# The first modulation of a two-block transformer kernel: shift half as direct products on TensorE, scale half on VectorE, and the first scaling ahead of the shift coefficient

## The reference, cut to what matters

```python
c_act = jax.nn.silu(c)                                          # (1, 1024)
mod = jnp.split(c_act @ w_ada[0] + b_ada[0], 9, axis=-1)        # mod[0] is the shift, mod[1] the scale, 1024 each
h = rms_norm(x, ffn1_norm[0]) * (1 + mod[1][:, None, :]) + mod[0][:, None, :]
x = x + 0.5 * (1 + mod[2])[:, None, :] * swiglu(h, ffn1_w_gu[0], ffn1_w_down[0])
```

## Time and profile before

| | us |
|---|---|
| median of 3 runs | 3137.26 (3135.42 to 3139.18) |
| profiled execution | 3139.89 |
| its span | 3138.1 |
| PE busy | 3095.8 |
| DVE busy | 1816.2 |
| ACT busy | 1201.4 |
| POOL busy | 1017.5 |

### The profile page before, as it was taken

One profiled execution on the slowest core, in us unless ns is written; L12 is line 12 of the kernel. 1 busy time (PEld: TensorE's weight loads), 2 busy tenths in 40 slices (PEclk: granted clock), 3 DMA queues, 4 the chain that ended last, 5 costly groups with the idle time before them and its releaser, 6 DMA issues.

```text
span 3138.1 us, 39389 instructions
## 1 busy us (share of the span) xinstructions
PE 3095.8 (99%) x14397; PEld 2511.1 (80%) x14397; DVE 1816.2 (58%) x2456; ACT 1201.4 (38%) x1818; POOL 1017.5 (32%) x722
## 2 busy tenths in 40 slices
PE   6999999999999999999999999999999999999999
PEld 5888877788888888877788888777888788888887
DVE  6555476665546443376665556446777868575443
ACT  4333246432223222246432234455433342443332
POOL 4995000069911830000079810000799101040000
PEclk8999999999999999999999999999999999999999
DMA  6665334267633643332266634212666345343332
GB/s 242 206 204 156 92 89 125 74 195 207 203 100 120 204 123 97 93 89 74 74 195 207 204 96 135 68 54 68 201 207 199 102 127 110 94 142 97 97 94 94
DMA packets 581129, 420.43 MB, mean 134 GB/s; under 512 B 41717, under 2 KB 541252, under 8 KB 579864
## 3 DMA queue, kind: packets, MB, share of 16 engines
q1 hardware_dynamic: 542116, 287.93, 31.4%
q0 software_dynamic: 35456, 124.01, 13.5%
q10 hardware_dynamic: 3444, 7.02, 0.8%
HBM read 413.10 MB, written 8.68 MB: 134 GB/s over the span
## 4 chain that ended last, share of the span: by engine, by line
PE 93%; DVE 4%; ACT 1%; issue 1%; DMA 1%; SPq 0%; DVEq 0%; ACTq 0%
PE bank L327 28%; PE bank L329 28%; PE bank L328 28%; PE bank L1574 2%; PE bank L1588 1%; PE bank L1615 1%; DVE w_lo L308 1%; PE bank L363 1%; PE bank L365 1%; PE bank L364 1%; DMA mod_w<-in_w_ada 1%; DVE tmp L457 1%; DVE h_lo L467 0%; PE bank L3136 0%; PE bank L417 0%
## 5 line engine op out<-in xcount | busy, mean ns | idle before, releaser
L327 PE MATMUL bank<-h_hi,w_hi 128*128 128x512 f32 x2624 | 1035.8, 395 | 4.9 <-DVE h_lo L467 3.1
L329 PE MATMUL bank<-h_hi,w_lo 128*128 128x512 f32 x2624 | 1023.8, 390 | 0.0
L328 PE MATMUL bank<-h_lo,w_hi 128*128 128x512 f32 x2624 | 1023.2, 390 | 0.0
L308 DVE TENSOR_TENSOR w_lo<-raw,w_hi 128x1024 fp32r<-128x1024 f32 x414 | 609.4, 1472 | 567.3 <-ACT w_hi L291 564.9
L291 ACT ACTIVATE w_hi<-raw 128x1024 fp32r<-128x1024 f32 x414 | 437.7, 1057 | 788.4 <-PE bank L329 788.3
L327 PEld LDWEIGHTS bank<-h_hi,w_hi 128*128 128x128 f32 x2624 | 492.1, 188 | 122.4 <-issue 10.9
L329 PEld LDWEIGHTS bank<-h_hi,w_lo 128*128 128x128 f32 x2624 | 492.0, 187 | 105.8
L328 PEld LDWEIGHTS bank<-h_lo,w_hi 128*128 128x128 f32 x2624 | 492.6, 188 | 100.4 <-issue 0.5
L760 POOL TENSOR_TENSOR mod_acc<-mod_acc,mod_w 128x1024 f32<-128x1024 f32 x168 | 446.8, 2659 | 14.7
L327 PE MATMUL bank<-hid_hi,w_hi 128*128 128x512 f32 (+1 forms) x1068 | 415.6, 389 | 3.9 <-DVE w_lo L308 3.3
L329 PE MATMUL bank<-hid_hi,w_lo 128*128 128x512 f32 (+1 forms) x1068 | 413.3, 387 | 0.0
(11 more groups left out here) (433 smaller groups left out, 3279.6 us busy)
## 6 DMA issues: line engine op xcount, KB each, us to landing
raw<-in_ffn_w_gu SPq DMA_DIRECT2D x176, 512.0 KB, 4.4
mod_w<-in_w_ada POOLq DMA_DIRECT2D x128, 512.0 KB, 3.9
mod_w<-in_mod_w POOLq DMA_DIRECT2D x96, 512.0 KB, 4.2
raw<-in_ffn_w_in SPq DMA_DIRECT2D x88, 512.0 KB, 3.8
raw<-in_ffn_w_down SPq DMA_DIRECT2D x64, 512.0 KB, 3.5
raw<-in_w_in SPq DMA_DIRECT2D x34, 512.0 KB, 3.7
raw<-in_ffn_w_out SPq DMA_DIRECT2D x32, 512.0 KB, 3.5
raw<-in_ffn_w_down SPq DMA_DIRECT2D x32, 384.0 KB, 3.1
```

Of the source, the lines that this page charges most:

```text
L308: loop(nc.vector.tensor_tensor(w_lo[:, u % 2, :], raw[:, u % 2, :], w_hi[:, u % 2, :].bitcast(F32), ALU.subtract), "split_lo", times)
L327: nc.tensor.matmul(dst, a_hi, b_hi, start=start, stop=False)
L328: nc.tensor.matmul(dst, a_hi, b_lo, start=False, stop=False)
L329: return nc.tensor.matmul(dst, a_lo, b_hi, start=False, stop=stop)
```

## The change

It does five things. (1) DVE accumulates only columns 1024 to 2047 of each chunk, the scale half. (2) The shift half of each chunk is multiplied on PE as it is: mod_direct makes 8 products of one column, with mod0_w as weights and cact[t] as the column, and adds them up over the chunks in bank 6. PE does chunks 0 to 4, norm_spread, chunks 5 and 6, the scale sums (mod_total), chunk 7, and then pe_later. (3) SP loads the last chunk in two halves, the scale half first; the shift half waits for chunk 0 to have landed, since it uses that chunk's semaphore. (4) DVE scales tile 0 between the scale coefficient and the shift coefficient; one of the two first split_lo stands between them, the other behind the first h_lo; DVE is one scaling ahead of its h_lo instead of two. ACT waits for the shift coefficient before its first rounding. (5) FIRST_PAIR has (1, 0) second instead of third.

```diff
--- before.py
+++ after.py
@@ -581,7 +581,7 @@
                     done(ins, "unit_used")
             turn.pe += 2
 
-        FIRST_PAIR = [(0, 0), (0, 1), (1, 0), (0, 2), (1, 1), (0, 3), (1, 2), (0, 4), (1, 3), (0, 5), (1, 4), (0, 6), (0, 7),
+        FIRST_PAIR = [(0, 0), (1, 0), (0, 1), (0, 2), (1, 1), (0, 3), (1, 2), (0, 4), (1, 3), (0, 5), (1, 4), (0, 6), (0, 7),
                       (1, 5), (1, 6), (1, 7)]
 
         def first_pair_pe(pe, key):
@@ -601,6 +601,8 @@
 
             for m in range(n):
                 wait(act, "norm_scaled", (key, m))
+                if key == PHASES[0] and m == 0:
+                    act.wait_ge(sg.sem("coef_ready"), at("coef_ready", "shift"))
                 done(nc.scalar.activation(dst_hi(m), tmp[:, m % 3, :], ACT.Identity,
                                           bias=0.0 if shift is None else shift(m)), "norm_hi", (key, m))
 
@@ -642,13 +644,20 @@
         def set_parts(key, s):
             return [j for t, j in mod_jobs(key) if t == s]
 
-        def mod_total(pe, s, j, bank):
+        def mod_direct(pe, t, j, bank, first):
+
+            for b in range(KT):
+                ins = nc.tensor.matmul(psum[bank][:, 8 * j + b:8 * j + b + 1], mod0_w[:, t, j * D + b * P:j * D + (b + 1) * P],
+                                       cact[:, t:t + 1], start=first and b == 0, stop=False, skip_group_check=True)
+            return ins
+
+        def mod_total(pe, s, j, bank, alone=True):
 
             wait(pe, "mod0_summed", (s, j))
             for b in range(KT):
                 ins = nc.tensor.matmul(psum[bank][:, 8 * j + b:8 * j + b + 1],
                                        mod_acc[:, j * D + b * P:j * D + (b + 1) * P], ones[:, 0:1],
-                                       start=True, stop=True, skip_group_check=True)
+                                       start=alone, stop=True, skip_group_check=True)
             done(ins, "mod_total", (s, j))
 
         def folds(n):
@@ -782,9 +791,13 @@
                 sp.dma_start(x_tok[:, t, :], d["x"][0, t * P:(t + 1) * P, :]).then_inc(sg.sem("x_loaded"), 16)
             wait(sp, "rows_cleared", "all")
             load_rows(sp, True)
-            for t in range(KT):
+            for t in range(KT - 1):
                 sp.dma_start(mod0_w[:, t, :], d["w_ada"][0, t * P:(t + 1) * P, 0:2 * D])\
                     .then_inc(sg.sem(f"mod0_loaded{t}"), 16)
+            last = d["w_ada"][0, (KT - 1) * P:KT * P, 0:2 * D]
+            sp.dma_start(mod0_w[:, KT - 1, D:2 * D], last[:, D:2 * D]).then_inc(sg.sem(f"mod0_loaded{KT - 1}"), 16)
+            sp.wait_ge(sg.sem("mod0_loaded0"), 16)
+            sp.dma_start(mod0_w[:, KT - 1, 0:D], last[:, 0:D]).then_inc(sg.sem("mod0_loaded0"), 16)
 
         def load_rows(sp, first):
             name = "rows_first" if first else "rows_loaded"
@@ -853,10 +866,16 @@
                     ins = nc.tensor.transpose(psum[m % 2][:, t * P:(t + 1) * P], x_tok[:, t, m * P:(m + 1) * P],
                                               ident[:, :])
                 done(ins, "x_turned", m)
-            norm_spread(pe, PHASES[0], 4)
+            wait(pe, "act_c", "c")
+            for t in range(KT - 1):
+                pe.wait_ge(sg.sem(f"mod0_loaded{t}"), 16)
+                mod_direct(pe, t, 0, 6, t == 0)
+                if t == 4:
+                    norm_spread(pe, PHASES[0], 4)
+            mod_total(pe, 0, 1, 3)
+            pe.wait_ge(sg.sem("mod0_loaded0"), 32)
+            done(mod_direct(pe, KT - 1, 0, 6, False), "mod_total", (0, 0))
             pe_later(pe)
-            mod_total(pe, 0, 1, 3)
-            mod_total(pe, 0, 0, 6)
 
         def pe_later(pe):
 
@@ -894,26 +913,24 @@
             take_rows(0)
             wait(dve, "shape_loaded", "all")
             wait(dve, "act_c", "c")
-            acc = mod_acc[:, 0:2 * D]
-            for t in range(KT - 1):
+            acc = mod_acc[:, D:2 * D]
+            for t in range(KT):
                 dve.wait_ge(sg.sem(f"mod0_loaded{t}"), 16)
                 if t == 0:
-                    ins = nc.vector.tensor_scalar(acc, mod0_w[:, t, :], cact[:, t:t + 1], None, ALU.mult)
+                    ins = nc.vector.tensor_scalar(acc, mod0_w[:, t, D:2 * D], cact[:, t:t + 1], None, ALU.mult)
                 else:
-                    ins = nc.vector.scalar_tensor_tensor(acc, mod0_w[:, t, :], cact[:, t:t + 1], acc, ALU.mult, ALU.add)
-                vstep(ins)
-                if t == 5:
+                    ins = nc.vector.scalar_tensor_tensor(acc, mod0_w[:, t, D:2 * D], cact[:, t:t + 1], acc, ALU.mult, ALU.add)
+                if t < KT - 1:
+                    vstep(ins)
+                else:
+                    done(ins, "mod0_summed", (0, 1))
+                if t == 3:
                     norm_invert(dve, PHASES[0])
-            t = KT - 1
-            dve.wait_ge(sg.sem(f"mod0_loaded{t}"), 16)
-            for j in (1, 0):
-                half = acc[:, j * D:(j + 1) * D]
-                done(nc.vector.scalar_tensor_tensor(half, mod0_w[:, t, j * D:(j + 1) * D], cact[:, t:t + 1], half, ALU.mult,
-                                                    ALU.add), "mod0_summed", (0, j))
-            for _ in range(LOOK):
-                split_lo(dve)
             mod_coef(dve, 0, [1], 3)
+            norm_scale(dve, PHASES[0], psum[4][:, :], 0, lambda m: x[:, m, :], gain_of(0))
+            split_lo(dve)
             mod_coef(dve, 0, [0], 6)
+            mark("coef_ready", "shift")
 
         def take_rows(t):
             n = 1 if t == 0 else ROW_TILES - 1
@@ -1350,8 +1367,13 @@
             kind, l = FFN[key]
             s = key[1]
             if key not in LAZY:
-                norm_scale_split(dve, key, 4, KT, lambda m: x[:, m, :], gain_of(s), shift_of(s),
-                                 lambda m: h_lo[:, m, :], lambda m: h_hi[:, m, :])
+                dst_lo, dst_hi = lambda m: h_lo[:, m, :], lambda m: h_hi[:, m, :]
+                for m in range(1, KT):
+                    norm_scale(dve, key, psum[4][:, :], m, lambda m: x[:, m, :], gain_of(s))
+                    norm_low(dve, key, m - 1, shift_of(s), dst_lo, dst_hi)
+                    if m == 1:
+                        split_lo(dve)
+                norm_low(dve, key, KT - 1, shift_of(s), dst_lo, dst_hi)
                 after_norm(dve)
             u0 = turn.dve - LOOK
             mark("pair_evac", (key, "base"))
```

## The result

| | before | after |
|---|---|---|
| median | 3137.57 us (11 runs) | 3146.0 us (11 runs) |
| ratio, 95% interval | | 1.0022 (1.0014 to 1.003) |
| profiled execution, its span | 3139.89, 3138.1 | 3143.53, 3141.7 |
| DVE busy | 1816.2 | 1794.3 |
| matrix instructions of PE | 14397 | 14509 |

The change makes the kernel slower by 8.4 us by the medians (9.1 in the second series; the ratios say 7 and 9); 10 was forecast. Ten of the eleven runs after lie between 3142.5 and 3149.4; one execution of 13919 us at a granted clock of 0.21 is a disturbance that the ratio leaves out.

A forecast was written before the change was run, and what follows sets the result against it. PE, busy for 99% of the span, was taken to bound the kernel. First dense product at 54.3 instead of 43.75 (+10.5), clock -0.5, all else 0: +10.0 on the median, 3147.3 us, range 3142 to 3151.5.

The forecast's parts named there:

- The step that was taken as deciding: PE's direct products: half clock from 21.9, 0.218 us per instruction, 3.5 us per chunk against loads every 2.5 us.
- (1): DVE's accumulation of w_ada chunks: half as wide, some 1.2 us saved per chunk, counted 0 because PE is not ready.
- (2): PE's 64 direct products replacing 8 sums: last direct product ends at 51.1, where the last sum ended at 40.8.
- (3): pe_later on PE: no longer hidden, its 3.2 us stand behind the last direct product and end at 54.3.
- (4): Tile 0 scaled before the shift coefficient: first h_lo 1.6 us after it instead of 2.3; gain 0.7 covered, counted 0.
- (5): New waits and queues on ACT and SP: cost 0; next raw loads land 4.4 us later, hidden.
- (6): Clock of the first dense products: half-clock stretch may shorten or lengthen, taken as -0.5 us, bounds -2.7 and +2.7.
- Rival A: PE keeps full clock through the direct products, last one at 37.4: result -5, 3132 us; chance 0.06.
- Rival B: Full clock lasts three to seven us longer on PE's direct products: +4 to +7, 3141 to 3144 us; chance 0.08.
- C: Direct products dearer beside DMA traffic, or half clock after 54.3 twice as long: +12 to +14, 3150 to 3152; chance 0.06.

The follow-up runs named there:

- direct3: The changed kernel with direct products for the first 3 chunks only, DVE summing the other shift chunks, norm_spread and pe_later ahead of the sums: 3136.97 us, ratio 0.9995 to before.
- direct5: The changed kernel with direct products for the first 5 chunks only, DVE summing the other shift chunks, norm_spread and pe_later ahead of the sums: 3142.13 us, ratio 1.0012 to before.
- direct_dense2: The changed kernel with two float32 products of 512 columns among each chunk's 8 direct products, 16 in all: 3147.35 us, ratio 1.0033 to before.
- after_again: The changed kernel itself, run once more in the second series: 3146.01 us, ratio 1.0028 to before.
- later_first: The changed kernel with pe_later moved from behind the last direct product to ahead of the scale sums: 3148.91 us, ratio 1.0037 to before.
- scale_first: The kernel before with only parts 4 and 5 of the change (DVE and ACT order, FIRST_PAIR): 3137.39 us, ratio 0.9997 to before.
- direct_filled: The changed kernel with 7 transposes of the identity into an unused bank among each chunk's 8 direct products: 3148.9 us, ratio 1.0035 to before.
- direct_dense: The changed kernel with one float32 product of 384 columns into an unused bank among each chunk's 8 direct products: 3156.36 us, ratio 1.0056 to before.
- dense_scale_first: The kernel before with scale_first's edit and PE's idle time filled with 10, 2 and 2 float32 products of 512 columns: 3133.53 us, ratio 0.9989 to before.
- before_filled: The kernel before with PE's idle time filled with 76, 12 and 16 transposes of the identity: 3134.13 us, ratio 0.9991 to before.
- filled_scale_first: The kernel before with scale_first's edit and PE's idle time filled with transposes of the identity: 3133.85 us, ratio 0.999 to before.

## Why the prediction was right

The step that was taken as deciding, which clock the direct products get, held: 64 products of one column at half clock for most of their time, longer than the loads, on a PE that DVE and ACT wait for. direct3, direct5 and the change show the loss growing with their number; direct_dense2 shows that at full clock PE has room for 13.7 us of other work beside them. The sizes came out less well, and in part by errors that cancel.

Term by term:
- (1) DVE's saving, counted 0: 0. It waits 14.49 us for PE.
- (2) The last direct product was to end at 51.1 and ended at 49.4. This is the term that was mis-sized, by 1.7 us, and that is the net of two errors. PE came to the first one 0.8 us later than reckoned. The 112 instructions of chunks 0 to 6 took 20.5 us and not 22.9, since full clock lasted for 3.4 us of them (21.12 to 24.6) and not 1.6; in after_again it was 3.3 us, in later_first 2.0. The half-clock rate was nearly right: 0.213 per instruction for the 32 at 35.79, for 0.218.
- (3) pe_later was to end 3.2 us behind the last direct product, and did (49.31 to 52.55). Of this 1.1 us is exposed, the rest lies beside DVE's and ACT's way to the first h_lo. It was not quite hidden in the kernel before, as the prediction has it: there DVE had summed the scale half at 33.15, and PE's sums began at 33.81, straight behind pe_later.
- (4) First h_lo 1.6 us after the shift coefficient, foretold; 51.46 less 49.85, measured 1.6. The second split cost nothing. scale_first has the 0.8 us that this order is worth where PE is not in the way.
- (5) The waits cost nothing ahead of the first products: the raw units were rounded at 33.26 and 34.76, as before. Ahead of the third unit PE waits 0.71 us for its split, 0.46 before.
- (6) The clock of the first dense products, taken as -0.5: from the first of them to the third unit PE took 14.19 us in before, 13.14 in after and 14.34 in after_again. So the term came out as -1.05 once and as +0.15 once. The reason that was given for its sign, no idle time ahead of them, stands in both and decides nothing.

Together 7.75 at the third unit, where 10.0 was forecast, and 8.4 and 9.1 in the medians; why the medians are that much above the places in the traces is open.

Rival A, full clock through the direct products, fell. PE is busy for 4.50 of 4.50 us between 25.0 and 29.5 and is granted 0.50. The Trainium skill ("TensorE: Matmul & The Clock Gate", section "HAM oscillation — how this bites in real kernels") gives as the rule that PE is to be left no long idle gaps if it is to keep its clock. That is not enough here: PE was left none from 21.12 on, and had half clock from 24.6 to 55.3; the measurement decides. Rival B came true in part: 1.8 us more of full clock than the forecast had, worth some 1.6 by its own price of 0.9 per us. C did not: 49 instructions from 24.6 to 34.9, most of them beside full DMA traffic (share 0.94 in the mean to 34.6), and 32 from 35.8 to 42.5, at a share of 0.00, took 0.21 us each alike.

## What to carry to other kernels

Price PE's instructions at the clock that they themselves will get: a run of one-column products with 128x128 float32 weights costs 0.213 us per instruction at half clock, nearly twice the 0.115 of full clock, even on a PE that is never idle. Before moving work to an idle engine, ask whether that engine's own queue stands between the last load and the first dependent result; here the idle time held three chunks and not eight. When single profiles are compared, look for the same group at different durations elsewhere before trusting the difference of the spans.

## What the runs showed of the hardware

- PE's granted clock fell and stayed at half under gapless runs of one-column products: alone (after), with a transpose between each two (direct_filled), and with one float32 product of 384 columns per 8 (direct_dense). It stayed full with two products of 512 columns per 8 (direct_dense2, until 49.8), under products of 512 columns alone (dense_scale_first), and under transposes alone in before_filled, 76 in 8.46 us. In filled_scale_first it had fallen at 19.7, ahead of the same 76 transposes, and came back at 22.8 under them.
- How long full clock lasted behind the transposes of x varied from run to run: it fell at 21.9 in before, where PE had been idle from 20.2 on, and at 24.6 in after and 23.0 in after_again, where PE never paused.
- Runs of the kernel before spread from 3135.0 to 3140.9 us in 27, and the mean granted clock of a run goes with its time: the 6 runs of that series at 0.994 took 3140.1 us in the mean, the 5 at 0.996 took 3136.5. Other series have the same order.
- At half clock a transpose between two one-column products costs 0.10 us, and in a run of its own 0.21 (filled_scale_first, 16 from 37.90 to 41.20, granted 0.50).
- The first 16 transposes of x took 0.23 us each in before and after, though the profile has the granted clock as 1.00 there, while the last 8 took 1.14 together. So how far that column holds ahead of 17 us is not settled; nothing here rests on it there.
- Filling PE's idle time with useless dense products made the kernel 4.0 us faster by the medians (ratio 0.9989, 0.998 to 0.9998).
